# Attention scores read the 64 key rows of their head directly, without a zero-padded copy of the keys

## The reference

```python
G = H // SWA_KV_HEADS                      # 3
s_loc = einsum('bnqkgd,bnpkd->bnkgqp', qb, kb) * d ** -0.5   # blocks i-1, i, i+1 of 128 keys
s_ctx = einsum('bnqkgd,bpkd->bnkgqp', qb, kc) * d ** -0.5    # all 256 context keys
p = softmax(concatenate([s_loc, s_ctx, s_sink], -1))
```

## Time and profile before

| | |
|---|---|
| median of 3 runs | 4207.72 us (4205.66 to 4210.34) |
| profiled execution, its own time | 4205.66 us |
| its span in the trace | 4203.8 us |
| PE busy | 3369.2 us (80%) |
| DVE, ACT, POOL busy | 1141.7, 948.9, 583.2 us |
| attention, layer 0 | first score 453.27, last result 624.41 us |
| SWA part of attention, layer 0 and layer 1 | about 451 to 552 and 2618 to 2692 us |

### The profile page before, as it was taken

How to read it: one execution, slowest core, us unless ns; L and a number is a source line. 1 busy time by engine, 2 the same in 40 slices (tenths; PEclk the granted TensorE clock), 3 DMA queues, 4 the chain that set the end, 5 groups by cost and what they waited for, 6 DMA issues and landing times. The chain is left out here.

```text
span 4203.8 us, 60180 instructions
## 1 busy us (share of the span) xinstructions
PE 3369.2 (80%) x22700; PEld 1942.8 (46%) x22701; DVE 1141.7 (27%) x2450; ACT 948.9 (23%) x1701; POOL 583.2 (14%) x648
## 2 busy tenths in 40 slices
PE   6699787956519999999990598989662999999991
PEld 2355566933304444444440354769431444444440
DVE  0242542432311111111116443634322111111115
ACT  1222442221102222222220232532110222222221
POOL 0010004220040000000005010032203000000003
PEclk8699998987659999999995699999775999999995
DMA  9510008021034898698867310000212599999955
GB/s 417 196 55 10 3 18 324 4 84 60 21 122 168 336 358 339 232 357 313 310 240 296 114 57 6 1 15 4 81 43 110 206 361 363 366 358 371 357 194 230
DMA packets 142744, 788.23 MB, mean 188 GB/s; under 512 B 16560, under 2 KB 36912, under 8 KB 105776
## 3 DMA queue, kind: packets, MB, share of 16 engines
q1 hardware_dynamic: 82976, 577.93, 34.9%
q0 software_dynamic: 37120, 125.89, 8.4%
q10 hardware_dynamic: 22464, 81.80, 4.8%
HBM read 649.09 MB, written 139.62 MB: 188 GB/s over the span
## 5 line engine op out<-in xcount | busy, mean ns | idle before, releaser
L1889 PE MATMUL psum<-arena 128*128 x2496 | 1105.5, 596 | 8.1 <-issue 8.1
L1889 PEld LDWEIGHTS psum<-arena 128*128 128x128 f32 x2496 | 463.0, 190 | 583.3 <-issue 583.3
L1900 PE MATMUL psum<-arena 128*128 x1248 | 550.5, 594 | 0.0
L726 PE MATMUL psum<-arena 128*128 128x480 f32 (+3 forms) x1088 | 400.9, 525 | 2.2 <-ACT arena L580 2.2
L1868 POOL DMA_INDIRECT arena<-h,arena x160 | 149.7, 935 | 1653.0 <-PE psum L1883 1638.6
L1900 PEld LDWEIGHTS psum<-arena 128*128 128x128 f32 x1248 | 230.7, 190 | 261.2 <-issue 261.2
L726 PEld LDWEIGHTS psum<-arena 128*128 128x128 f32 x1088 | 206.8, 193 | 176.3 <-issue 166.7
L1883 PE MATMUL psum<-arena 128*128 128x128 f32 x1280 | 169.6, 276 | 142.4 <-DMA arena<-h,arena 142.4
L1958 ACT ACTIVATE arena<-psum 128x256 f32<-128x256 f32 x156 | 60.2, 386 | 778.8 <-PE psum L1889 778.8
L1883 PEld LDWEIGHTS psum<-arena 128*128 128x128 f32 x1280 | 149.9, 143 | 185.4 <-DMA arena<-h,arena 144.2
L1999 DVE COPY arena<-psum 128x512 f32<-128x512 f32 x156 | 107.9, 692 | 450.7 <-PE psum L1900 450.7
(11 more groups left out here) (313 smaller groups left out, 3730.2 us busy)
## 6 DMA issues: line engine op xcount, KB each, us to landing
arena<-in_w_gu SPq DMA_DIRECT2D x130, 2048.0 KB, 8.6
arena<-in_w_dn SPq DMA_DIRECT2D x130, 1024.0 KB, 12.0
y_slots<-arena ACTq DMA_DIRECT2D x156, 512.0 KB
arena<-in_ada SPq DMA_DIRECT2D x24, 2048.0 KB, 17.2
y_slots<-arena SPq DMA_DIRECT2D x8, 4096.0 KB, 34.6
arena<-xres SPq DMA_DIRECT2D x32, 512.0 KB, 6.7
arena<-in_w_gdn SPq DMA_DIRECT2D x6, 1536.0 KB, 14.0
arena<-in_w_out SPq DMA_DIRECT2D x2, 4096.0 KB
```

Source lines behind the costliest of these rows:

```text
L726: last = nc.tensor.matmul(bank(n, wide), lhsT[:, k], rhs[:, k], start=(k == 0), stop=(k == DK - 1))
L1889: last = nc.tensor.matmul(psum[:, 2 + r, :], xT[:, r, k * P:(k + 1) * P], W[:, bass.ds(slot + k * 2 * DE, 2 * DE)], start=(k == 0), stop=( ...
L1900: last = nc.tensor.matmul(psum[:, (LEFT, RIGHT)[n][r], :], hT[:, r, j * P:(j + 1) * P], W[:, bass.ds(slot + DK * 2 * DE + j * D + n * 512, ...
```

## The change

The array `kz`, its four filling instructions per layer, their semaphore and PE's wait for it go. The SWA score takes the 64 partitions of its key head from `skT` and the same 64 partitions of `sqT`. The matmul streams the same columns, over 64 rows in place of 128.

```diff
-                kz = sbuf(st, "kz", [P, SWA_KV, NTOK])
-                kz_ready = S("kz_ready")
...
                             if swa:
                                 g, j = h // 3, h % 3
-                                q, k = sqT[:, j, i * P:(i + 1) * P], kz[:, g]
+                                q, k = sqT[64 * g:64 * g + 64, j, i * P:(i + 1) * P], skT[64 * g:64 * g + 64, :]
...
-                        pe.wait_ge(kz_ready, 2 * SWA_KV)
                         score(0)
...
-                        for g in range(SWA_KV):
-                            nc.vector.memset(kz[64 - 64 * g:128 - 64 * g, g], 0.0).then_inc(kz_ready, 1)
...
-                        for g in range(SWA_KV):
-                            nc.scalar.copy(kz[64 * g:64 * g + 64, g], skT[64 * g:64 * g + 64, :]).then_inc(kz_ready, 1)
```

## The result

The changed kernel takes 4320.31 us (median of 4 runs, 4314.23 to 4323.74) against 4209.03 us (4205.66 to 4212.18) for the kernel before on the same chips: a ratio of 1.0266, 95% interval 1.0251 to 1.0282. It is 111 us slower; forecast was +1.25 us, in a range that ended at 4217. The profiled execution has a span of 4318.3 us with a mean granted clock of 0.864, where the one before had 4203.8 and 0.894.

The account below looks back on a forecast made before the run. The prediction took a loop over PE, DVE and ACT to bound SWA, with no engine full. Start -3.55 us and switches +4.8 gave +1.25, so 4207.72 became 4209.0 us, range 4203 to 4217.

Parts of the forecast that it names:

- The start: Start of attention: without copies, memsets and PE's wait, the first score comes 1.78 us earlier per layer, -3.55 us in all.
- The table load: ACT's 1.28 us load at the start of attention moves up with the first score and stays hidden.
- The price of the switches: SWA scores: 0.20 us per change between 128 and 64 rows, 0.40 per head on the loop, +4.8 us in all.
- the switch out: From 64-row score back to 128-row values: its 0.20 us mostly hides where PE waits for ACT's copy.
- rival C: SWA stretches: 64-row scores or empty array at switches drop the clock to 1.2 GHz, some +90 us, 4300; chance 0.03.
- C's sentence on idle time: SWA stretches: the clock follows how busy PE is, so a few per cent more idle time would lower it.
- Rival B: SWA units: the switch out counts too, up to +20.5 us, 4228.2; chance 0.17 beyond 8.4 us.
- A: SWA loop: switches hidden altogether or nearly, only the start's gain remains, 4204.2 us; chance 0.14.

Follow-up runs that it names:

- mla_first_64: The changed kernel with MLA's heads first and SWA's last: 4255.0 us, ratio 1.0120 to the kernel before.
- late_heads_64: The kernel before with heads 3 to 5 scoring over 64 rows, heads 0 to 2 over 128 padded, filling and wait kept: 4263.08 us, ratio 1.0126.
- padding_kept_64: The kernel before with filling instructions and wait kept, but all SWA scores over 64 rows from unpadded keys: 4323.47 us, ratio 1.0271.
- probe: The kernel before plus seven TensorE-only stretches; second: 60 matmuls over 64 rows, third: 128 and 64 rows alternating; 4653.94 us with the added phase.
- switch_only: The kernel before, 128-row scores, with one small 64-row matmul of 4 columns ahead of each SWA score: 4222.95 us, ratio 1.0034.

## Why the prediction was wrong

*The start* was right: 1.84 us per layer measured, 1.78 forecast. The table load stayed hidden.

*The price of the switches* was right where it can be read at full clock, which is in mla_first_64 and late_heads_64. In late_heads_64 the two transposes before the first 64-row score are followed after 505.35 - 505.03 = 0.32 us, which is twice 0.11 and 0.10 of empty array, and that score's first pair takes 505.88 - 505.35 = 0.53, 0.10 over 0.43. A head costs 0.39 us more in layer 0 and 0.41 in layer 1, forecast 0.40, and the idle times before values are 0.56, 0.16, 0: the switch out is hidden where I said. By these numbers the change at full clock would give 6 x (0.39 + 0.41) - 2 x 1.84 = +1.1 us. That is an estimate; no run kept the clock up throughout.

*The step that failed* is rival C, "The clock falls", and in it the sentence "the delta rule's preparation is all 64 x 64 products with many switches and has 0.97". It made a price of some +90 us into a chance of 0.03, and the sum was made with durations at full clock throughout. What the runs showed in its place is that SWA with 64-row scores is held at 0.50 for all of its length (with the padding and the late start kept too, in padding_kept_64), and that 64-row matmuls of 128 columns alone stay at 0.50 for 50 us (`probe`, row 2).

The sentence also misreads the trace. The products are 5502 of the 5564 PE instructions of the window 660 to 860, but "many switches" is wrong: the timeline goes between 64 and 128 rows only 18 times in these 200 us, where the 60 SWA units have two switches each. And the products aren't 64-row work of the kind that the scores became. Two rows of the kernel before, a window and a place of the timeline:

```profile
740.00:780.00 40.00, 40.00 (x1310) 38.12 (x1308) 18.94 (x36) 11.26 (x25) 16.92 (x21) 1.00 0.02 4
```

```profile
801.66 1.61 PE L1208 MATMUL psum<-arena 64*64 64x64 f32 x48
803.11 0.80 PE L1244 MATMUL psum<-arena 64*64 64x64 f32 x21
```

Here 48 products start within 803.11 - 801.66 = 1.45 us, 0.030 each, while 64 columns at the rate of the full-clock scores (512 in 0.43 us) would take 0.054. In the kernel they take both halves of the rows and of the columns by turns, so products run beside each other, while in the scores nothing runs in the other 64 rows. That this is what keeps the clock up is argued; no run here tests it.

C's sentence on idle time does not fit either: in the changed kernel PE is never idle in SWA, and the clock stays down. With this many switches the 64 rows are needed for the loss: with 128-row scores (switch_only) the clock is up. What the switches add is open.

The size follows roughly from C's own working. It gave +90 us for SWA at half clock; measured are 6 x 10.24 = 61.4 and 6 x (21.15 - 12.24) = 53.5 us (a head of layer 1 takes 2758.06 - 2736.91 = 21.15 in the changed kernel), less some us in the two stages that were at half clock before as well. C had left the switches out of its price, and a switch costs more at half clock: in the third stretch of `probe` a pair of 256 columns follows the last after 250.67 - 249.52 = 1.15 us, of which the columns take 0.86, so 0.29 in place of 0.20, and with PE the bound there is no wait left for it to hide in. For 60 units with two switches each that is 35 us, an estimate and more than the some 20 to 25 us that C's +90 lacks; the other way, values do not quite double (ten take 1.17 us from start to start at full clock and 573.40 - 571.22 = 2.18 here).

*Rival B* fell: there is no sign that the switch out was exposed at full clock. *A* fell as well, as a head did take 0.39 to 0.41 us more.

The Trainium skill, TensorE: Matmul & The Clock Gate, section Why this matters for your kernels, advises to keep TensorE busy continuously for the full clock. Here 50 us of unbroken matmuls over 64 rows stayed at 0.50, so the trace differs: being busy without a break is not enough.

## What to carry to other kernels

Zeros that fill a matmul up to 128 rows can pay for themselves: here four small instructions per layer are the price of scores over 128 rows, with which the 83.0 and 55.5 us of SWA in the earlier trace rows run at 2.4 GHz; with scores over 64 rows the two attention stages take 61.7 and 50.1 us longer. Before replacing a full matmul by a partial one of the same columns, look whether the stage needs it to bring the clock up, and try the edit with a stage that starts cold. When a row of another stage is taken as evidence on the clock, count its switches, and compare how its matmuls fill the array, not their shape's smaller side alone.

## What the runs showed that was not expected

- PE busy for 100% of 130 us at a granted clock of 0.50, in the changed kernel, and for 50 us in a stretch of plain 64-row matmuls.
- Two states for the same instructions, of which the high one was lost in both layers of the run that had it: a head of 64-row scores at 16.53 us and 1.00, or at 26.38 us and 0.50.
- Half of the matmuls over 64 rows: at 0.50 for 69 us when every one switches, at 0.95 when they come in unbroken fours.
- 96 rows in place of 128 in half of the scores: the full clock came some 7 us later in each layer. The stages lost 2.4 and 2.0 us, the kernel 0.26%, most of it in a place that isn't known.
